# Six embedding products per layer computed inside two earlier norms and kept in DRAM

## The chip, the cores and the metric

The kernel runs on one core of one Trainium2 chip. The metric is the device time of one execution in microseconds, and less is better. One launch computes the whole network for a sequence of 512 tokens.

## The reference

`x` is 512 tokens of 1024 channels. A first block mixes tokens in three ways (gated linear attention, windowed attention, pooling), gates and adds the three, and projects; a conv feed-forward follows; behind each stands a norm of what was computed. A second network has an mLSTM layer, a per-layer embedding (PLE) addition, a shared key and value projection, a dilated attention layer, and another PLE addition. Cut to what the change touches:

```
x = x + rmsnorm(merged @ w_out, norm_mix_post)          # the norm of mixing
f = conv_ffn(rmsnorm(x, norm_ffn_pre), ...)
x = x + rmsnorm(f, norm_ffn_post)                       # the norm of the feed-forward
...
def ple_add(h, p_l, norm_g, w_gate, w_proj):
    gate = sigmoid(rms_norm(h, norm_g) @ w_gate)        # 1024 x 1024
    return h + (p_l @ w_proj) * gate                    # p_l is an input: 512 x 256
```

The product `p_l @ w_proj` depends on inputs alone.

## The kernel before, in words

Activations lie transposed, channels on partitions and 512 tokens along the free dimension, so 1024 channels are 8 tiles of 128x512. Every fp32 product is three fp32r matmuls: each operand is split into a high part (a rounded copy) and a low part (what the rounding left), and PE adds high times high, high times low and low times high (`passes`, L386). A block is a weight of 128x128; a tile with k blocks takes 3k matmuls of 512 columns.

All weights come through one stream. SP loads units of 8 blocks (512 KB) into 3 raw buffers (`Loads`, L299), ACT rounds a unit into `WH` (`High`), DVE subtracts to get `WL` (`Low`), both in 5 slots, and PE uses the units in the order in which `_layout` packed them. There is no planner: each engine runs its own program, written by hand, and all five walk the same list of tiles (`tile`, `first`, `tokens4`, `taken`). At each block an engine calls `prepare` (L200), which brings its share of the stream up to 3 units ahead (4 for ACT); so weights are prepared only between the other instructions of that engine, in its program order. `later` lets small pieces that were put off (norm sums, ropes) run at fixed points. PE has eight PSUM banks: a ring `mp` of 3, or 7 where the other uses rest, and `SB` for the side work.

Four stages matter here.

*A norm behind a projection* (`pe_post` L649, `v_post` L1056, `a_post` L1703). ACT copies the last product tile to SBUF and squares the copy, POOL adds the square to `SQS`, PE sums over partitions (`pe_columns`: 4 small fp32 products), ACT and DVE make the reciprocal root, PE spreads it over a tile (`pe_row`), ACT copies that to `RT`. Then DVE, for each of 8 tiles: scales `F` by `RT` into `TT` (L1067), adds it to `X` (L1070), and, one tile later, subtracts `HH` from the scaled `X` for the low part `HL` (`v_low`, L1030); ACT makes `HH` and the squares for the next norm, POOL adds them.

*The opening behind it* (`first`, L415, and `tokens4`, L428). The first tiles of the next projection run k-outermost over several banks, so PE can use tile k of `HH` and `HL` as soon as it is there: 6 up-projection tiles behind mixing, 4 value tiles behind the feed-forward.

*A residual* (`residual`, L840, L1357, L1892): 8 tiles of an output projection; DVE adds each to `X`, waits for ACT's `HH` of the same tile, and makes `HL` at once.

*The PLE stage* (`ple`, L845, L1372, L1906): 3 gate tiles k-outermost (`pg`), 4 embedding products (`pw`, 2 blocks each), then 5 gate tiles with the last 4 products between them. For each tile DVE multiplies by the norm row (`v_half_tanh`, L1039), ACT takes tanh, DVE multiplies by the product in PSUM, adds to `X`, waits for ACT's high part, makes the low part, and only then goes on. The second PLE stage has no high and low parts, as it is the end.

## Time and profile before

| what | value |
|---|---|
| median of 3 runs | 1577.84 us (1574.33 to 1579.94) |
| the profiled execution | 1574.86 us, span 1572.9 us |
| mean granted TensorE clock | 0.963 of full |
| busy: PE, DVE, ACT, POOL | 1467.1, 929.2, 594.9, 162.2 us |
| data moved | 123.78 MB read, 2.10 MB written |

Busy times are sums over the instructions of an engine, and PE's are modelled, so a busy PE isn't PE at its peak. Where an engine is not the one that others wait for, its idle time costs nothing. All times within the trace count from the start of the span.

### The profile page before, as it was taken

How to read it: one execution, taken by the hardware profiler on the slowest of the kernel's cores; microseconds unless marked ns; L12 is line 12 of the kernel's file. 1: busy time of each engine (PE TensorE's matmuls, PEld its weight loads, DVE VectorE, ACT ScalarE, POOL GpSimd, SP SyncE). 2: the span in 40 equal slices, each digit the busy share in tenths (PEclk: the TensorE clock that was granted, in tenths of full speed). 3: DMA queues.
4: the chain of work that ended last, by engine and by line, in shares of the span. 5: the costliest groups of instructions: out<-in, count | busy, mean ns of one | idle time of the engine just before them, and what ended most of it. 6: DMA issues, size and time to landing. Idle time of an engine off the chain costs nothing.

```text
span 1572.9 us, 17894 instructions
## 1 busy us (share of the span) xinstructions
PE 1467.1 (93%) x7104; PEld 1186.8 (75%) x7104; DVE 929.2 (59%) x1273; ACT 594.9 (38%) x892; POOL 162.2 (10%) x124
## 2 busy tenths in 40 slices
PE   6998989899998989999999899899999999998898
PEld 5876767678876768888888678577888778776676
DVE  5443756555343689617884458445455757887654
ACT  5232543433234323322323352334444443556441
POOL 3300010120212200000001210000001101110010
PEclk9999999999998999999999899899999999999899
DMA  6220212122341213332333122211233242111221
GB/s 210 81 68 27 96 53 68 54 68 70 119 147 54 81 50 110 123 94 80 97 101 100 51 69 83 78 54 54 61 104 103 70 125 77 54 54 41 66 82 54
DMA packets 35971, 127.03 MB, mean 81 GB/s; under 512 B 4128, under 2 KB 4784, under 8 KB 35888
## 3 DMA queue, kind: packets, MB, share of 16 engines
q1 hardware_dynamic: 35888, 125.89, 25.8%
q8 instruction: 56, 0.92, 0.2%
q14 instruction: 27, 0.22, 0.0%
HBM read 123.78 MB, written 2.10 MB: 80 GB/s over the span
## 4 chain that ended last, share of the span: by engine, by line
PE 47%; DVE 12%; ACT 5%; issue 2%; DMA 0%; POOL 0%; DVEq 0%; ACTq 0%; SPq 0%
PE ps L191 47%; DVE WL L145 2%; DVE TT L157 2%; DVE PB L145 1%; DVE QK L157 1%; ACT L188 1%; DVE SS L157 1%; DVE TH L145 1%; ACT SS L188 1%; DVE sm L163 1%; DVE X L145 1%; ACT TH L188 1%; DVE HL L157 1%; DVE CT L157 1%; ACT WH L175 0%
## 5 line engine op out<-in xcount | busy, mean ns | idle before, releaser
L191 PE MATMUL ps<-HH,WH 128*128 128x512 f32 x1208 | 496.6, 411 | 32.1 <-DVE WL L145 21.1
L191 PE MATMUL ps<-HH,WL 128*128 128x512 f32 x1208 | 478.7, 396 | 0.0
L191 PE MATMUL ps<-HL,WH 128*128 128x512 f32 x1208 | 478.6, 396 | 0.0
L145 DVE TENSOR_TENSOR WL<-raw,WH 128x1024 fp32r<-128x1024 f32 x222 | 294.1, 1332 | 82.6 <-ACT WH L175 74.3
L191 PEld LDWEIGHTS ps<-HH,WH 128*128 128x128 f32 x1208 | 232.0, 192 | 90.0 <-issue 22.0
L175 ACT CAST WH<-raw 128x1024 fp32r<-128x1024 f32 x222 | 230.2, 1043 | 167.0 <-PE ps L191 128.7
L191 PEld LDWEIGHTS ps<-HH,WL 128*128 128x128 f32 x1208 | 231.6, 192 | 50.8
L191 PEld LDWEIGHTS ps<-HL,WH 128*128 128x128 f32 x1208 | 232.5, 192 | 47.9 <-issue 2.0
L191 PE MATMUL ps<-PH,WH 128*128 128x512 f32 x432 | 174.3, 404 | 6.4 <-DVE TT L157 3.4
L191 PE MATMUL ps<-PL,WH 128*128 128x512 f32 x432 | 170.5, 395 | 0.0
L191 PE MATMUL ps<-PH,WL 128*128 128x512 f32 x432 | 170.4, 394 | 0.0
L145 POOL TENSOR_TENSOR SQS<-SQS,SQ 128x512 f32<-128x512 f32 x56 | 81.3, 1452 | 825.4 <-ACT SQ L188 824.5
L145 DVE TENSOR_TENSOR TH<-ps,RS 128x512 f32<-128x512 f32 x100 | 68.6, 686 | 75.7 <-PE ps L191 70.3
L191 PEld LDWEIGHTS ps<-PH,WH 128*128 128x128 f32 x432 | 82.4, 191 | 27.6 <-DVE TT L157 4.2
L191 PEld LDWEIGHTS ps<-PH,WL 128*128 128x128 f32 x432 | 82.5, 191 | 17.8
L191 PEld LDWEIGHTS ps<-PL,WH 128*128 128x128 f32 x432 | 82.6, 191 | 16.2
L188 ACT ACTIVATE TH<-TH 128x512 f32<-128x512 f32 x48 | 30.3, 632 | 111.0 <-DVE TH L145 111.0
L157 DVE SCALAR_TENSOR_TENSOR CT<-TH,cv,CT 128x511 f32<-128x511 f32 x88 | 66.1, 751 | 3.1
L188 ACT ACT_TABLE_LOAD x49 | 62.9, 1283 | 10.2 <-DMA X<-in_xT 6.2
L169 DVE RECIPROCAL sm<-sm 128x4 f32<-128x4 f32 (+1 forms) x60 | 10.1, 171 | 93.6 <-ACT sm L188 91.1
L157 DVE SCALAR_TENSOR_TENSOR HL<-X,cv,HH 128x512 fp32r<-128x512 f32 x48 | 48.7, 1024 | 22.8 <-ACT HH L188 22.8
L191 PE MATMUL ps<-WH,HH 128*128 128x512 f32 (+1 forms) x128 | 49.6, 387 | 12.9 <-DVE WL L145 8.6
(194 smaller groups left out, 1500.9 us busy)
## 6 DMA issues: line engine op xcount, KB each, us to landing
raw<-in_wall SPq DMA_DIRECT2D x222, 512.0 KB, 3.6
X<-in_xT SPq DMA_DIRECT2D x8, 512.0 KB, 6.1
out_T<-X SPq DMA_DIRECT2D x8, 256.0 KB, 2.0
pt<-in_pT SPq DMA_DIRECT2D x2, 512.0 KB, 3.9
DM<-in_dm SPq DMA_DIRECT2D x1, 640.0 KB, 4.4
CS<-in_cs SPq DMA_DIRECT2D x1, 512.0 KB, 5.3
plw<-in_plw SPq DMA_DIRECT2D x1, 256.0 KB, 7.6
lvm<-in_lvm SPq DMA_DIRECT2D x1, 192.0 KB, 8.0
```

The lines of the kernel that those rows point to most:

```text
L145: return self.put(None if self.e is None else self.e.tensor_tensor(out, x, y, op))
L157: return self.put(self.e.scalar_tensor_tensor(out=out, in0=x, scalar=s, in1=y, op0=op0, op1=op1))
L163: return self.put(None if self.e is None else self.e.tensor_reduce(out, x, AX_X, op))
L169: return self.put(None if self.e is None else self.e.reciprocal(out, x))
L175: return self.put(None if self.e is None else self.e.copy(out, x))
L188: return self.put(self.e.activation(out, x, f, **kw))
L191: return self.put(None if self.e is None else self.e.matmul(out, l, r, start=start, stop=stop, skip_group_check=True))
```

## The change

Six of the eight embedding products of each layer (`EARLY = 6`) move out of the PLE stages: those of layer 0 into the norm of mixing, those of layer 1 into the norm of the feed-forward. The embedding `p` is loaded and split early for that (`early`). ACT copies each product to SBUF (`PW`), SP writes the six to DRAM (`kept`, 1.5 MB a layer) and reads them back (`PWR`) in front of the PLE stage. In the two norms the last square goes straight to PE without POOL's addition, mixing squares straight from PSUM, DVE reads the norm row from PSUM, and `ahead` lets ACT and DVE prepare weights inside the loop. The opening behind mixing has 4 tiles and no longer 6. PLE stages lose their k-outermost opening, and residuals and PLE stages make the low part one tile later. `_layout` follows the new order; the number of units is the same.

```diff
+    def ahead(self, m, n):
+        at = (self.blk + n * max(m - 2, 0)) // 8
+        self.prepare(at, at + NW - 1)
...
+        pes = [at("pe0", [P, 2, T], F32, o2), at("pe1", [P, 2, T], F32, ar + 24576)]
+        PW = [at("PW0", [P, EARLY, T], F32, ar + 26112), at("PW1", [P, EARLY, T], F32, ar + 16384)]
+        PWR = at("PWR", [P, EARLY, T], F32, ar)
+        kept = nc.dram_tensor("kept", [2, P, EARLY, T], F32, kind="Internal").ap()
...
-        def pe_post(p, st):
-            pe_columns(p, (SB[4], ("nc", st)), [(SQS, S.pool, ("sqs", st, 7))], [free("sqs", st)])
+        def pe_post(p, st, layer):
+            p.tile(("pw", layer, 0), O_e[layer])
+            pe_columns(p, (SB[4], ("nc", st)), [(SQS, S.pool, ("sqs", st, 6)), (sq_(st, 7), S.act, ("sqs in", st, 7))],
+                       [free("sqs", st), free("Q", (st, 7))])
+            p.tile(("pw", layer, 1), O_e[layer])
             pe_row(p, SB[4], ("nr", st), col_("post", st), ("post col", st), [free("COL", ("post", st))])
+            for m in range(2, EARLY):
+                p.tile(("pw", layer, m), O_e[layer])
...
+            def ple(layer, H, st, nxt):
+                for m in range(EARLY, 8):
+                    p.tile(("pw", layer, m), O_p[layer], SB[m - EARLY])
+                p.soon.append(pe_norm(p, st))
                 for m in range(8):
+                    p.tile(("pg", layer, m), H)
                 if nxt:
                     p.soon.append(pe_norm(p, nxt))
...
-            p.first([("up", 0, j, o) for j in range(3) for o in range(2)], H_ffn, [p.next_bank() for _ in range(6)])
+            p.first([("up", 0, j, o) for j in range(2) for o in range(2)], H_ffn, [p.next_bank() for _ in range(4)])
...
-            p.tokens4([("vt", t) for t in range(4)], H_kv, [p.next_bank() for _ in range(3)] + [SB[0]], early=True)
+            p.tokens4([("vt", t) for t in range(4)], H_kv, [SB[2], SB[3], p.next_bank(), p.next_bank()], early=True)
...
         def v_post(v, st, F, post, nxt, gain):
+            v.tile(2)
             v_column(v, ("post col", st), col_("post", st))
+            for m in range(1, 3):
+                v.tile(2)
             for m in range(8):
+                v.ahead(m, 4)
                 v.take("T", (st, m))
-                v.wait_ge(S.act, "post row", st)
+                v.wait_ge(S.pe, "nr", st)
...
-                v.scalar_tensor_tensor(tt_(st, m), F[:, m, :], c(post, m), rt_("post", st), MUL,
+                v.scalar_tensor_tensor(tt_(st, m), F[:, m, :], c(post, m), ps("nr", st), MUL,
...
+                if 3 <= m < EARLY:
+                    v.tile(2)
...
+            def early(layer):
+                for k in range(2):
+                    hi, lo = O_e[layer][k][0:2]
+                    v.wait_ge(S.act, "pe hi", layer, k)
+                    v.wait_ge(S.early[layer], "early")
+                    v.tensor_tensor(lo, pes[layer][:, k, :], hi.bitcast(F32), SUB).then_inc(("pe", layer, k))
...
-                    v_low(v, nxt, m, gain, HH, HL)
-                v.soon.append(v_norm(v, nxt))
+                    if m:
+                        v_low(v, nxt, m - 1, gain, HH, HL)
+                v_low(v, nxt, 7, gain, HH, HL)
...
                     v_half_tanh(v, tg, st)
-                    if 1 <= m <= 4:
-                        v.tile(2)
+                    if nxt and m:
+                        v_low(v, nxt, m - 1, "norm_kv", PH, PL)
                     v.take("T", tg)
                     v.wait_ge(S.act, "tanh", tg)
-                    v.wait_ge(S.pe, *tw)
...
+                    if m < EARLY:
+                        v.wait_ge(S.again[layer], "again")
+                        v.scalar_tensor_tensor(tt_(*tg), th_(*tg), 1.0, PWR[:, m, :], ADD, MUL).then_inc(("pt", layer, m), free("TH", tg))
...
+        def a_keep(a, layer, m):
+            a.wait_ge(S.pe, "pw", layer, m)
+            a.copy(PW[layer][:, m, :], ps("pw", layer, m)).then_inc(("pw", layer, m), free("pw", layer, m))
...
             for m in range(8):
+                a.ahead(m, 4)
...
+                if m + 3 < EARLY:
+                    a.tile(2)
+                    a_keep(a, layer, m + 3)
...
+                a_square(a, "mix post", m, ps("f", m), ("sqs", "mix"))
                 a.copy(FA[:, m, :], ps("f", m)).then_inc(("f", m), free("f", m))
-                a.wait_ge(S.act, "f", m)
-                a_square(a, "mix post", m, FA[:, m, :], ("sqs", "mix"))
...
+            def keep(layer):
+                s.wait_ge(S.act, "pw", layer, EARLY - 1)
+                s.dma_start(kept[layer], PW[layer]).then_inc("kept", sig=S.kept[layer], by=16)
...
             s.dma_start(pts[layer], a_in["pT"][layer]).then_inc("p", sig=S.p[layer], by=16)
+            s.wait_ge(S.kept[layer], "kept")
+            s.dma_start(PWR, kept[layer]).then_inc("again", sig=S.again[layer], by=16)
```

`keep(0)` stands behind the opening's weights in SP's queue, `keep(1)` behind the value tiles'; `load_p`, whose lines end the diff, stands in front of each residual. SP also loads `p` twice more (0.5 MB each). ACT's and DVE's `head` and ACT's `early(1)` wait for the writes before they reuse the memory.

## Rows read from the trace of the kernel before

**Rows 1.** The page, busy us, share of the span and instructions of each engine
```profile
PE 1467.1 (93%) x7104; PEld 1186.8 (75%) x7104; DVE 929.2 (59%) x1273; ACT 594.9 (38%) x892; POOL 162.2 (10%) x124
```

**Rows 2.** Windows: us, busy us (xcount) of PE, PEld, DVE, ACT, POOL; granted clock, DMA share, GB/s
```profile
497.20:508.20 11.00, 3.28 (x17) 2.96 (x17) 3.79 (x7) 5.37 (x9) 1.26 (x1) 0.65 0.00 0
...
508.20:546.00 37.80, 35.86 (x144) 29.06 (x145) 27.05 (x25) 14.01 (x19) 11.30 (x7) 0.92 0.25 84
...
546.00:645.00 99.00, 91.68 (x404) 75.65 (x404) 86.30 (x121) 29.07 (x39) 0.00 (x0) 0.97 0.26 80
...
884.00:924.20 40.20, 29.65 (x114) 24.29 (x114) 29.05 (x30) 16.70 (x24) 12.53 (x8) 0.79 0.12 41
...
1200.50:1285.40 84.90, 80.86 (x361) 66.51 (x359) 47.46 (x49) 34.69 (x46) 10.71 (x8) 0.98 0.31 93
...
1503.10:1567.60 64.50, 59.96 (x256) 48.28 (x254) 28.65 (x36) 17.13 (x22) 3.94 (x3) 0.95 0.20 70
```

**Rows 3.** Timeline (start, us), norm behind w_out
```profile
491.79 0.59 ACT L175 COPY FA<-ps 128x512 f32<-128x512 f32 x1 [3.25 <-PE ps L191]
...
497.23 0.58 ACT L175 COPY FA<-ps 128x512 f32<-128x512 f32 x1 [3.25 <-PE ps L191]
...
498.55 1.26 POOL L145 TENSOR_TENSOR SQS<-SQS,SQ 128x512 f32<-128x512 f32 x1 [4.13 <-ACT SQ L188]
...
499.87 1.23 PE L191 MATMUL ps<-ones,SQS 128*128 128x1 f32 x8 [2.67 <-POOL SQS L145]
...
501.75 2.04 PE L191 MATMUL ps<-ident,sm 128*128 128x128 f32 x8 [0.66 <-DVE sm L169]
...
503.83 0.58 ACT L175 COPY RT<-ps 128x512 f32<-128x512 f32 x1 [2.44 <-PE ps L191]
...
504.52 0.75 DVE L157 SCALAR_TENSOR_TENSOR TT<-FA,cv,RT 128x512 f32<-128x512 f32 x1 [2.91 <-ACT RT L175]
```

**Rows 4.** Timeline, end of the opening that follows, and the up projections
```profile
524.88 3.49 DVE L157 SCALAR_TENSOR_TENSOR HL<-X,cv,HH 128x512 fp32r<-128x512 f32 x2
...
528.30 3.48 DVE L145 TENSOR_TENSOR WL<-raw,WH 128x1024 fp32r<-128x1024 f32 x3
...
549.55 0.69 DVE L145 TENSOR_TENSOR TH<-ps,RS 128x512 f32<-128x512 f32 x1 [2.03 <-ACT RS L175]
...
570.44 1.22 DVE L145 TENSOR_TENSOR WL<-raw,WH 128x1024 fp32r<-128x1024 f32 x1
...
571.80 0.76 PE L191 MATMUL ps<-HH,WH 128*128 128x512 f32 x1 [6.66 <-DVE WL L145]
```

**Rows 5.** Timeline, two matmuls in a row on PE, 2 us into that opening
```profile
510.04 0.63 PE L191 MATMUL ps<-HL,WH 128*128 128x512 f32 x1
...
510.46 0.63 PE L191 MATMUL ps<-HH,WL 128*128 128x512 f32 x1
```

**Rows 6.** Timeline, first embedding layer
```profile
1216.70 0.95 PE L191 MATMUL ps<-ones,SQS 128*128 128x1 f32 x8
...
1218.99 1.05 PE L191 MATMUL ps<-ident,sm 128*128 128x128 f32 x8
...
1250.12 0.69 DVE L145 TENSOR_TENSOR TH<-ps,RS 128x512 f32<-128x512 f32 x1 [0.22 <-PE ps L191]
...
1256.63 0.68 DVE L145 TENSOR_TENSOR TH<-ps,RS 128x512 f32<-128x512 f32 x1
...
1263.85 0.50 PE L191 MATMUL ps<-WH,PH 128*128 128x512 f32 x1 [1.53 <-DVE TH L145]
```

**Rows 7.** Timeline, last residual, POOL and DVE at once
```profile
1493.22 1.34 POOL L145 TENSOR_TENSOR SQS<-SQS,SQ 128x512 f32<-128x512 f32 x1 [3.04 <-ACT SQ L188]
1493.32 0.68 DVE L145 TENSOR_TENSOR X<-X,ps 128x512 f32<-128x512 f32 x1
```

**Rows 8.** The page, DMA issues: count, KB each, median us to landing
```profile
raw<-in_wall SPq DMA_DIRECT2D x222, 512.0 KB, 3.6
X<-in_xT SPq DMA_DIRECT2D x8, 512.0 KB, 6.1
```

More of the change, by code:

```diff
@@ L64, in __init__ @@
         self.p = [p0, p1]
+        self.early = [e0, e1]
+        self.kept = [kept0, kept1]
+        self.again = [again0, again1]
         self.work = [self.pe, self.dve, self.act, self.pool]
@@ L954, in pe_program @@
                     for o in range(2):
-                        if half == 0 and jj < 3:
+                        if half == 0 and jj < 2:
                             p.taken()
@@ L1533, in dve_program @@
                     v.tile(8)
+                if m == 4:
+                    early(0)
             v.mark("merged")
             v_post(v, "mix post", FA, "mix_post", "ffn", "ffn_pre")
-            v.first(8, 6)
+            v.first(8, 4)
             v.mark("fb")
@@ L1551, in dve_program @@
                     for o in range(2):
-                        if half == 0 and jj < 3:
+                        if half == 0 and jj < 2:
                             v.taken()
@@ L1567, in dve_program @@
                     v.tile(11)
+                    if half == 1 and m == 4:
+                        early(1)
                     if half == 1:
@@ L1843, in head @@
                 a.wait_ge(S.act, "acol")
+                a.wait_ge(S.kept[1], "kept")
                 if h:
@@ L1903, in residual, with ple @@
                     a_square(a, nxt, m, X[:, m, :], ("sqs", last))
-                a.soon.append(a_norm(a, nxt, use))
-            def ple(layer, nxt, last):
-                a.first(8, 3)
-                for m in range(4):
+            def ple(layer, st, nxt, last, use):
+                for m in range(EARLY, 8):
                     a.tile(2)
+                a.soon.append(a_norm(a, st, use))
                 for m in range(8):
-                    if m < 3:
-                        a.taken()
-                    else:
-                        a.tile(8)
+                    a.tile(8)
                     a_tanh(a, ("pg", layer, m))
-                    if 1 <= m <= 4:
-                        a.tile(2)
                     if nxt:
@@ L2018, in act_program, with early @@
                 a.activation(HH[:, m, :], X[:, m, :], ACT.Copy, scale=0.5).then_inc(("mg hi", m))
+            def early(layer):
+                for k in range(2):
+                    hi = O_e[layer][k][0]
+                    a.wait_ge(S.early[layer], "early")
+                    if layer:
+                        a.wait_ge(S.kept[0], "kept")
+                    a.copy(hi, pes[layer][:, k, :]).then_inc(("pe hi", layer, k))
             a.mark("fa")
@@ L2049, in act_program @@
                     for o in range(2):
-                        if half == 0 and jj < 3:
+                        if half == 0 and jj < 2:
                             a.taken()
@@ L2065, in act_program @@
                     a.tile(11)
+                    if half == 1 and m == 4:
+                        early(1)
                     if half == 0:
@@ L2323, in sp_program @@
                 s.tile(8)
-            s.first(8, 6)
+            for m in range(EARLY):
+                s.tile(2)
+            s.first(8, 4)
+            keep(0)
             for half in range(2):
-                for _ in range(22 - 6 * (half == 0)):
+                for i in range(22 - 4 * (half == 0)):
                     s.tile(8)
+                if half == 1:
+                    s.wait_ge(S.kept[0], "kept")
+                    s.dma_start(pes[1], a_in["pT"][1]).then_inc("early", sig=S.early[1], by=16)
                 for m in range(8):
                     s.tile(11)
+            for m in range(EARLY):
+                s.tile(2)
             s.tokens4(8)
+            keep(1)
             s.wait_mark("a")
@@ L2457, in _layout @@
         if half == 0:
-            side_by_side(*((up, j * P + o) for j in range(3) for o in (0, 2816)))
-        for j in range(half * 11 or 3, (half + 1) * 11):
+            side_by_side(*((up, j * P + o) for j in range(2) for o in (0, 2816)))
+        for j in range(half * 11 or 2, (half + 1) * 11):
             form(up, j * P)
```

105 lines of the change are left out of this document (50 added, 55 removed).

## The prediction

> **What bounds the kernel.** I began with the page's busy times: PE is busy 1467.1 of 1572.9 us and nothing else comes near [rows 1], so what matters is where PE waits or runs slowly. The list of waits and the timeline put most of that into few stages. I cut the span into windows at their borders, measured from the end of one projection to the start of the next use [rows 2]. The reader should see in them that the granted clock is 0.65 in the 11 us of the norm behind mixing, where PE does 3.3 us of work, and 0.79 in the whole stretch behind the feed-forward; and that DVE, not PE, is nearly full there (29.1 of 40.2 us) and is at 86.3 of 99.0 us in the first half of the up projections.
>
> **The pace.** Two tiles of 24 matmuls end 5.44 us apart [rows 3], so a matmul takes 0.227 us at the clock of 2.4 GHz. At 1.2 GHz two in a row start 0.42 us apart [rows 5]. The matmuls of the change are the same ones in another order. Six products are 36 matmuls, 8.2 us, in each layer. The change gains what PE's order fills or removes.
>
> **The norm of mixing, now.** The last tile of w_out ends at 497.2 [rows 3]. ACT copies (0.58), squares, POOL adds (1.26), and the sums start at 499.87, 2.7 us late. They take 1.23 and the row 2.04, both at the lower clock. ACT copies the row, DVE starts at 504.52. PE starts the opening only at 508.2. DVE's loop of 8 tiles runs until 524.88 + 3.49 = 528.4, so 23.9 us [rows 3, 4]. That is more than 24 instructions of 0.75: the last two take 3.49 together [rows 4]; seven are stretched like that, each while POOL adds.
>
> **The norm of mixing, after.** Product 0 fills 497.2 to 498.6; the last square goes first on ACT and is there by 497.9. The sums are twice as many, 2 x 0.95 at the full clock [rows 6], to 500.5. Product 1 to 501.8 covers the root, also if a weight cast and a table load keep it until 501.1. The row takes 1.05 [rows 6], to 502.9. DVE reads it from PSUM and starts 1.6 us earlier. Products 2 to 5 are 24 matmuls, to 508.3. The first low part is due by 506.8 (DVE's start plus the 3.5 us that it takes now), so PE doesn't stop, and its clock should not have fallen.
>
> DVE's loop has the same 24 instructions and, by `ahead`, four low weights (indices 4 to 7 from the first unit of the products; 0 to 3 are ready). Three of them take 3.48 us [rows 4], so 1.16 each and 4.6 together: the loop takes 28.5 us, to 531.4. ACT's additions (6 copies at 0.58, four casts) lie beside it: ACT is busy 14 of 37.8 us in the opening now [rows 2]. POOL loses one addition. The last k-step is 12 matmuls, 2.7 us, to 534.2. PE alone would be through 32 blocks (21.8 us) at 530.1, so **DVE becomes the bound of the opening** and PE stalls 4.1 us in pieces of up to 1.6, in front of the steps that a low weight delays. The next norm adds 2.7 as now, to 536.9.
>
> Now DVE has six tiles waiting for that norm. It works from 549.55 to 570.44 before it comes to a weight, and PE, with three units in hand (16.3 us), starves for 6.66 us until 571.80 and comes back at the lower clock [rows 4]. With four tiles DVE takes 20.9 x 4/6 = 13.9 us, and PE has 28 blocks, 3.5 units, 19.1 us. The starvation goes. What is late next is nothing in this stage: 18 tiles take PE 97.9 us, and DVE's work for all 22 is 86.3 us [rows 2]. It ends at 536.9 + 97.9 = 634.8 against 644.5: **9.7 us earlier**, with 8.2 us of products done besides.
>
> **The norm of the feed-forward.** The same steps: DVE starts 5.7 us in, 28.5 for its loop, 2.7 for the last step, 36.9 against 40.2 us [rows 2], so **3.3 us earlier**. DVE had done its weights behind the loop; now they come inside it.
>
> **The PLE stages.** In the first one a tile costs DVE 6.5 us (1250.12 to 1256.63), more than PE's 5.44: norm multiply, wait for tanh, two steps, wait for ACT's high part (0.8), low part, weight (2.3, beside POOL) [rows 6]. After the change the low part fills the wait for tanh and the wait for the high part is gone: 1.15 to 2.3 + 0.7 + 0.75 + 0.7 + 0.7, at most 5.2 us. PE bounds it. From the end of the residual: 2 products 2.7, norm 2.0, 8 tiles 43.5, value tiles 21.8, sums 0.95, together 71.0 against 84.9 us [rows 2]: **13.9 us**. Of these, 8.2 are the products; the rest are waits for DVE, the 1.5 us in front of 1263.85 among them [rows 6]. The p0 norm loses its cover of 24 matmuls, but its sums stand after half of gate tile 0, 5.4 us behind the residual, and DVE, ACT and POOL need 0.69 + 0.72 + 0.62 + 1.34, 3.4 us.
>
> In the second, 2.7 + 2.0 + 43.5 = 48.2 against 64.5 us [rows 2]: **16.3 us**. Here the three banks of the present opening were held by DVE, which is 6.5 us for two residual tiles where PE needs 5.44; with the wait for ACT gone it needs 5.0 to 6.0, and 5.4 us of other PE work stand behind it. The tail is the same.
>
> **Edits costed at nothing.** The early split of `p` (4 instructions of 0.6 us a layer on ACT and DVE) lies under w_out and the down projection, where PE's tiles take 5.44 and 33 x 0.227 = 7.5 us; uncovered it would be 1.3 us each. The four transfers of 1.5 MB are unlike any row; the nearest give 86 to 145 GB/s (0.52 MB in 6.1 or 3.6 us) [rows 8], so 11 to 18 us each. The writes stand behind weights that are already issued. In front of a residual `p` and the products (2.1 MB, 14.5 to 24.4 us) stand ahead of the next weights, with 3 units, 16.3 us, in hand. I take the fast value, since the raw loads are the same kind: no stall. The slow end is 8.1 us at each place. The products are needed only behind the residual, which is 8 x 5.44 = 44 us in layer 0 and half of that in layer 1.
>
> **The sum.** 9.7 + 3.3 + 13.9 + 16.3 = 43.2 us. From it I take 2 us for a fall of the clock in one of the openings' stalls (14 matmuls at 0.42 cost 2.9; stalls of 1.5 us leave it up [rows 6], one of 6.66 does not), so 41. The profiled execution took 1574.86 us, 0.2% under the median, so 1533.9 for it and **1536.8** beside 1577.84.
>
> A rule that bears on DVE's loop: while POOL added, a DVE instruction that reads PSUM kept its 0.68 us [rows 7]. The Trainium skill, "SBUF — State Buffer", "Who interferes with whom", says that a VectorE instruction with at most one SBUF input does not contend with GpSimd. The trace agrees. Two of the seven slow ones in the loop are scalings that will read PSUM, at 1.05 us each; by the rule the sum would be up to 4 us better, by the row's pattern (the next instruction waits instead) nothing.
>
> **Rivals.** (a) *The openings fall into the lower clock.* Each has three or four stalls now; if each of six costs 2.9 us, it is 15 more than I took: 1552. Against it: gaps of 1.5 us left the clock up. The Trainium skill, "TensorE: Matmul & The Clock Gate", "A second HAM failure mode: psum-queue depth-cycling", tells of a kernel whose short idles between groups made the clock swing; the trace doesn't show that for gaps this short.
> (b) *The order of the low parts shortens nothing*, so PLE 0 stays at 6.5 us a tile: 8 x 1.06 = 8.5 us, 1545. For it: DVE is the releaser there now. Against it: 0.8 us of each tile is a wait for ACT.
> (c) *The reloads starve PE*, at the slow rate: 2 x (8.1 + 2 for the clock) = 20 us, 1557. The same mechanism turns to **slower than before** when each place costs 20.5 us, which is 2.1 MB in 36.8 us, under 57 GB/s. At 45 GB/s it is 30 us each, 1597. Against it: the slowest row is 86, and the page's raw loads land in 3.6 us.
> (d) *It doesn't do what it says*: DVE's backlog behind the openings eats their 13 us and DVE-bound PLE stages the rest but for the last one: about 1573.
>
> **Chances.** Forecast 0.64, its own range 1531 to 1543; (a) 0.12; (b) 0.11; (c) 0.07 short of the turn, 0.03 beyond it; (d) 0.03. The 80% range takes the forecast, (a) mostly and (b): 1529 to 1554. About 0.3% is what a measurement of this kernel can tell from no change. Faster 0.94; same 0.03; slower 0.03.
>
> **What would show it.** PE without a gap from the last tile of w_out to the end of product 5; DVE's loop of 28 us; no gap behind the four up tiles; norm multiplies 5.44 us apart in PLE 0. I am wrong if PE stalls more than 5 us in an opening, if the clock in one is under 0.9, or if a weight load lands over 16 us after a reload was issued.

## The result and the profile after

Measured beside each other on one chip, the changed kernel takes **1534.69 us** (median of 4 runs, 1533.44 to 1535.64) where the kernel before takes 1576.09 (4 runs, 1574.14 to 1579.94): 0.9736 of its time, with a 95% interval of 0.9718 to 0.9754. The forecast was 1536.8, range 1529 to 1554. The profiled span went from 1572.9 to 1533.0 us.

The page of the changed kernel, first the engines [rows 1], then its DMA issues [rows 8]:

```profile
PE 1453.6 (95%) x7120; PEld 1179.2 (77%) x7120; DVE 913.5 (60%) x1277; ACT 602.2 (39%) x908; POOL 171.3 (11%) x122
...
kept<-PW SPq DMA_DIRECT2D x2, 1536.0 KB, 7.6
...
PWR<-kept SPq DMA_DIRECT2D x2, 1536.0 KB, 7.6
```

PE does the same work in 13.5 us less busy time (about 35 matmuls fewer run at the lower clock, 0.42 us apart instead of 0.23, which is half of it), and the other 26 us are waits that are gone. (The sixteen matmuls more are the second sums of the two norms.) The windows of the changed kernel, with the columns of [rows 2]:

```profile
497.00:507.80 10.80, 10.80 (x61) 9.32 (x60) 5.07 (x9) 8.52 (x14) 0.00 (x0) 1.00 0.09 36
507.80:533.20 25.40, 23.05 (x99) 17.78 (x98) 22.44 (x22) 12.60 (x19) 11.13 (x7) 1.00 0.32 91
533.20:633.70 100.50, 99.84 (x450) 82.92 (x449) 86.92 (x119) 30.76 (x40) 0.00 (x0) 1.00 0.33 103
633.70:876.80 243.10, 241.31 (x1058) 199.27 (x1057) 139.70 (x174) 69.51 (x86) 9.25 (x6) 0.99 0.34 102
876.80:910.90 34.10, 33.54 (x160) 27.33 (x158) 27.18 (x31) 19.74 (x30) 10.79 (x7) 1.00 0.28 71
910.90:997.00 86.10, 76.31 (x337) 61.91 (x335) 53.77 (x70) 30.92 (x41) 0.00 (x0) 0.94 0.31 102
1191.50:1262.20 70.70, 70.70 (x325) 58.92 (x325) 41.38 (x49) 33.53 (x45) 10.44 (x8) 1.00 0.33 98
1479.30:1527.70 48.40, 48.36 (x220) 39.65 (x219) 25.57 (x32) 13.42 (x18) 2.33 (x2) 1.00 0.23 71
```

PE fills the norm behind mixing completely (10.80 of 10.80 us, where it had 3.28 of 11.00 [rows 2]) and the granted clock is 1.00 in every stage that the change meant to reach. It also fills both embedding stages. But one row is out of line: 910.9 to 997.0 has PE busy 76.3 of 86.1 us at a clock of 0.94, and that stage had not been part of the forecast. Put beside the windows of before, border by border, the whole span comes out (the forecast column is before the 2 us that the forecast held back for a fall of the clock):

```
stage                                     before   after    change   forecast
norm behind mixing, ups of half 0          147.8   136.7     -11.1      -9.7
downs of half 0, half 1                    239.0   243.1      +4.1       0
norm of the feed-forward, first V tiles     40.2    34.1      -6.1      -3.3
rest of attention stage a, to the heads     78.4    86.1      +7.7       0
heads and first residual                   197.9   194.5      -3.4       0
first embedding stage                       84.9    70.7     -14.2     -13.9
second layer's attention                   217.7   217.1      -0.6       0
second embedding stage                      64.5    48.4     -16.1     -16.3
ahead of the norm of mixing, and the tail  502.5   502.3      -0.2       0
sum                                       1572.9  1533.0     -39.9     -43.2
```

(The border at 645.0 [rows 2] lies 0.5 us behind the last matmul of that stage, so PE's own share of the first two lines is -10.6 and +3.6.) The sum is near the forecast one, but two losses nobody had forecast, 11.8 us, stand against gains larger than forecast.

One of these gains is in no edited stage, the 3.4 us between the heads and the first residual. Its windows, of the kernel before and of the changed one:

```profile
1002.60:1200.50 197.90, 195.94 (x889) 154.42 (x890) 99.59 (x136) 78.24 (x125) 8.06 (x6) 0.95 0.22 65
```

```profile
997.00:1191.50 194.50, 191.68 (x889) 151.74 (x890) 91.88 (x135) 78.28 (x124) 9.58 (x6) 0.97 0.24 76
```

The same 889 matmuls take PE 4.3 us less, with a granted clock of 0.97 and not 0.95, while its idle time grows from 2.0 to 2.8 us. So these 3.4 us are the clock, not waits; why it is higher here, no run shows.

**The openings.** The timeline of the changed kernel (start, us; in brackets the idle time before it and what ended it), to be read against [rows 3, 4, 5]:

```profile
502.59 0.75 DVE L163 SCALAR_TENSOR_TENSOR TT<-FA,cv,ps 128x512 f32<-128x512 f32 x1 [1.70 <-PE ps L197]
...
508.38 2.32 DVE L151 TENSOR_TENSOR WL<-raw,WH 128x1024 fp32r<-128x1024 f32 x1
...
513.76 1.59 POOL L151 TENSOR_TENSOR SQS<-SQS,SQ 128x512 f32<-128x512 f32 x1 [1.91 <-ACT SQ L194]
...
514.13 0.73 DVE L163 SCALAR_TENSOR_TENSOR TT<-FA,cv,ps 128x512 f32<-128x512 f32 x1
514.89 1.00 DVE L151 TENSOR_TENSOR X<-X,TT 128x512 f32<-128x512 f32 x1
...
524.07 0.47 PE L197 MATMUL ps<-HH,WH 128*128 128x512 f32 x1 [1.35 <-DVE HL L163]
...
526.69 1.62 DVE L163 SCALAR_TENSOR_TENSOR HL<-X,cv,HH 128x512 fp32r<-128x512 f32 x2
...
642.35 0.50 PE L197 MATMUL ps<-PH,WH 128*128 128x512 f32 x1 [1.79 <-DVE PL L151]
...
643.63 0.63 PE L197 MATMUL ps<-PH,WL 128*128 128x512 f32 x1
...
646.62 0.59 PE L197 MATMUL ps<-PH,WH 128*128 128x512 f32 x1
647.04 0.40 PE L197 MATMUL ps<-PL,WH 128*128 128x512 f32 x1
```

DVE starts at 502.59, 1.9 us earlier than before, and ends its loop at 528.3: 25.7 us, where the forecast was 28.5. The scaling of 514.13, which reads PSUM, keeps its 0.73 us beside POOL's addition of 513.76, and the addition of 514.89, which reads SBUF twice, takes 1.00 where one free of POOL takes 0.69; POOL's addition ends at 515.35, so it looks as if DVE waits for what is left of it. The last rows are the first loss. In the first down tile PE is 1.79 us early for DVE's last low part PL, and 1.3 us after it resumes, eight matmuls follow each other at 0.42 us instead of 0.23 (643.63 to 647.04). That is 1.8 + 8 x 0.19 = 3.3 of the 3.6 us. (The traces of low_undo, row_copy, open6, again4, gate3 and bank below have the same wait, 1.63 to 1.86 us, no_ahead has 0.44 and early4 none; the slow matmuls behind it are in bank alone.)

Why DVE is late shows in its list of waits over the up projections (533.2 to 633.7 us):

```profile
DVE PL L151 <- ACT PH L181: 6.9, 10, 0.7
DVE sm L175 <- ACT sm L194: 3.8, 1, 3.8
DVE TH L151 <- ACT RS L181: 2.0, 1, 2.0
```

DVE is busy for 86.9 of these 100.5 us, waits 12.7 us for ACT, and not once for PE. So it has no time in this stage to catch up: it comes out of the opening behind PE and stays behind to the last tile.

**Stage a.** The second loss, in the same timeline:

```profile
967.84 0.68 DVE L151 TENSOR_TENSOR TH<-ps,RS 128x512 f32<-128x512 f32 x1
968.58 0.80 PE L197 MATMUL ps<-WH,HH 128*128 128x512 f32 x1 [4.66 <-DVE TH L151]
...
973.90 0.68 DVE L151 TENSOR_TENSOR TH<-ps,RS 128x512 f32<-128x512 f32 x1
974.63 0.80 PE L197 MATMUL ps<-WH,HH 128*128 128x512 f32 x1 [4.41 <-DVE TH L151]
```

These are the second four value tiles of the attention. They don't wait for data: each needs a PSUM bank, and the bank is one that DVE has yet to read (PE starts 0.06 and 0.05 us after DVE's reads at 967.84 and 973.90 end). The banks are handed out in a ring, and the change takes twelve products out of later stages and puts them into earlier ones, so the ring stands elsewhere when stage a begins. Nobody edited this line.

### The profile page after: what moved, and what is told of

It is laid out like the page before. It is cut to its first block, busy times and chain, and to the rows that moved or that the text cites. A ratio compares the mean times of both kernels' runs of the same rounds, so it can differ in the third digit from the quotient of the medians.

```text
span 1533.0 us, 17910 instructions
## 1 busy us (share of the span) xinstructions
PE 1453.6 (95%) x7120; PEld 1179.2 (77%) x7120; DVE 913.5 (60%) x1277; ACT 602.2 (39%) x908; POOL 171.3 (11%) x122
## 4 chain that ended last, share of the span: by engine, by line
PE 72%; DVE 18%; ACT 6%; issue 3%; DMA 1%; POOL 1%; DVEq 0%; SPq 0%; ACTq 0%
PE ps L197 71%; DVE WL L151 4%; DVE CT L163 2%; DVE TT L163 1%; DVE TH L151 1%; ACT L194 1%; DVE PB L151 1%; DVE QK L163 1%; DVE SS L163 1%; DVE sm L169 1%; DVE CT L158 1%; ACT SS L194 1%; DVE HL L163 1%; ACT PH L181 1%; DVE gqks L151 1%
## 5 line engine op out<-in xcount | busy, mean ns | idle before, releaser
L197 PE MATMUL ps<-HH,WH 128*128 128x512 f32 x1208 | 494.2, 409 | 18.1 <-DVE WL L151 12.7
L151 DVE TENSOR_TENSOR WL<-raw,WH 128x1024 fp32r<-128x1024 f32 x222 | 281.7, 1272 | 75.5 <-ACT WH L181 74.8
L197 PEld LDWEIGHTS ps<-PL,WH 128*128 128x128 f32 x426 | 81.5, 191 | 16.1
L194 ACT ACTIVATE HH<-X,cv 128x512 fp32r<-128x512 f32 x48 | 34.7, 723 | 47.4 <-DVE X L151 47.4
```

The costliest lines, as they stand in the source:

```text
L151: return self.put(None if self.e is None else self.e.tensor_tensor(out, x, y, op))
L194: return self.put(self.e.activation(out, x, f, **kw))
L197: return self.put(None if self.e is None else self.e.matmul(out, l, r, start=start, stop=stop, skip_group_check=True))
```

## The experiments

Each kernel is the changed one with one edit, except the first. The ratios are to the kernel before, measured beside it on the same chip, with 95% intervals. Stage times are cut at landmarks that every trace has: *dn0*, from the last copy of `FA` to the first of `FB` (opening, ups and first down tile); *va0*, from the last addition of `FB` to the first copy of `VA`; *heads*, from there to the heads' first row product; *res a*, to the last addition of the residual; *ple 1*, to the next layer's first `VT`; *res z*, to the last addition of the second residual; *end*, from there.

```
us           dn0    va0   heads  res a  ple 1  res z   end    span
before     154.9   41.6   77.0  197.9   85.3  221.6  65.4  1572.9
after      145.8   35.4   84.8  194.5   71.2  218.6  51.7  1533.0
low_only   157.8   41.9   76.7  199.2   81.2  217.6  62.4  1566.4
low_undo   145.9   35.4   84.5  196.5   71.2  221.2  53.3  1535.3
row_copy   148.3   38.8   85.0  194.4   71.2  218.9  51.7  1536.2
early4     143.3   37.2   76.9  195.8   75.7  221.0  55.9  1536.5
open6      151.0   35.4   85.3  196.0   71.2  221.2  51.6  1538.6
no_ahead   146.2   35.7   85.8  195.6   71.2  218.6  51.7  1534.9
again4     145.8   35.4   84.6  203.8   71.2  227.3  55.3  1553.0
bank       145.9   35.4   73.5  195.6   71.2  218.6  51.7  1522.4
dnfirst    164.1   35.4   85.1  195.3   71.2  218.2  51.7  1528.8
gate3      145.9   35.3   84.6  196.5   75.2  219.1  53.9  1540.0
both       164.1   35.4   73.5  197.4   71.2  219.6  51.7  1523.6
both5      164.1   35.3   73.6  197.5   71.2  217.2  51.6  1518.4
```

A stage that an edit doesn't touch can differ by up to 3 us between these kernels: *res a* goes from 194.4 to 197.5, *dn0* is 2.9 us longer in low_only than before, and *res z* is 219.6 and 217.2 in *both* and *both5*, which are the same kernel. In *res a* 7 to 24 matmuls run at the lower clock, in places that move. *va0*, *ple 1* and *end* are steadier, within 0.4 us where nothing touches them. So a stage's change is read only where it is over that or where a row of the timeline carries it.

### The order of the low parts: alone, and taken back

Alone, in the kernel before (each low part one tile later):

```diff
                     v.tensor_tensor(X[:, m, :], X[:, m, :], ps("res", st, m), ADD).then_inc(("x " + nxt, m), free("res", st, m))
-                    v_low(v, nxt, m, gain, HH, HL)
+                    if m:
+                        v_low(v, nxt, m - 1, gain, HH, HL)
+                v_low(v, nxt, 7, gain, HH, HL)
...
+                    if nxt and m:
+                        v_low(v, nxt, m - 1, "norm_kv", PH, PL)
                     v.take("T", tg)
```

> The kernel before, with nothing but the low parts of residuals and embedding stages made one tile later. My account (the wait for ACT's high part inside DVE's chain, 0.8 us a tile, made DVE the bound): the first embedding stage, 84.9 us from the end of the residual to the end of the value tiles, has 240 matmuls, 96 for the values and 3 us of norm, 79.3 us in all, so it can gain up to 5.5, and the second, 64.5 us for 240 matmuls and 2.0, up to 8: 6 to 13 us less together, 1563 to 1570. Rival (the order of the low parts does nothing by itself, only the moved products count): 1575 to 1578.

Measured: 1568.3 us (1567.54 to 1568.57), ratio 0.9933 [0.9913, 0.9954]. Some 10.6 us by the ratio and 6.5 by the traces. *ple 1* gives 4.1 us, *res z* and *end* together 7.0; *dn0*, untouched, is 2.9 longer. So in the kernel before, the order alone shortens the embedding stages.

The same edit taken out of the changed kernel:

> The kernel after, with the low parts back in their old place. My account: the 8 tiles of the first embedding stage go back from 5.44 to 6.5 us, 8.5 us longer, and in the last residual DVE needs 6.5 us for two tiles where PE needs 5.44, of which part is hidden behind the two products; 8.5 to 13 us more, 1543 to 1548. Rival (with the products gone from the stage DVE has room enough, since it no longer meets them): within 2 us of 1534.7.

Measured: 1539.62 us (1537.06 to 1542.34), ratio 0.9753 [0.9729, 0.9776]: 2.3 us slower than with the order by the spans, 4.9 by the medians, and the intervals of the two ratios overlap. It lies between the two ranges expected. The first embedding stage is 71.2 us as with the order. The timeline of this kernel, two gate tiles of that stage and the next norm:

```profile
1219.21 0.68 DVE L151 TENSOR_TENSOR TH<-ps,RS 128x512 f32<-128x512 f32 x1
...
1225.70 0.68 DVE L151 TENSOR_TENSOR TH<-ps,RS 128x512 f32<-128x512 f32 x1
...
1485.37 1.34 PE L197 MATMUL ps<-ones,SQS 128*128 128x1 f32 x8 [4.12 <-POOL SQS L151]
```

DVE takes 6.5 us a tile again, as before [rows 6], and with the new order 5.44 (below). PE doesn't feel it, and has no wait in this stage: eight tiles let DVE fall some 8 us behind, and it seems that there are banks enough to hold that. My reading of [rows 6], that a tile's DVE time sets the stage, was wrong for the changed kernel. The loss is at the second residual, where the sums wait 4.12 us for a chain that begins with DVE's last addition; the changed kernel has no wait there, and *res z* and *end* together are 4.2 us longer.

### The norm's row: read from PSUM, or from a copy

```diff
-                v.wait_ge(S.pe, "nr", st)
+                v.wait_ge(S.act, "post row", st)
...
-                v.scalar_tensor_tensor(tt_(st, m), F[:, m, :], c(post, m), ps("nr", st), MUL,
-                                       MUL).then_inc(("post", st, m), *([free("nr", st)] * (m == 7)))
+                v.scalar_tensor_tensor(tt_(st, m), F[:, m, :], c(post, m), rt_("post", st), MUL,
+                                       MUL).then_inc(("post", st, m), *([free("RT", ("post", st))] * (m == 7)))
```

> The kernel after, but DVE reads the norm row of the two post norms from SBUF, where ACT copies it first, as before. The copy puts 0.6 us in front of DVE's loop. If a DVE instruction with one SBUF input never waits for POOL, and one with two does, the seven slow instructions of a loop come back in full: the loop goes from 25.7 to about 28.5 us, PE's stalls in the opening behind mixing from 2.3 to about 5 us, and the total is 3 to 7 us more (1538 to 1542). If the slowing has to do with time alone (a POOL addition costs DVE 1 us whatever it runs), only the copy is seen: 0.6 us twice, 1535 to 1536.

Measured: 1542.64 us (1537.94 to 1543.32), ratio 0.9765 [0.9741, 0.979]; by the span 3.2 us slower. The timeline of this kernel, two of the three scalings in the mixing norm that meet an addition of POOL, and that addition for the second:

```profile
509.42 1.78 DVE L163 SCALAR_TENSOR_TENSOR TT<-FA,cv,RT 128x512 f32<-128x512 f32 x1
...
524.88 1.59 POOL L151 TENSOR_TENSOR SQS<-SQS,SQ 128x512 f32<-128x512 f32 x1 [3.83 <-ACT SQ L194]
...
525.24 1.78 DVE L163 SCALAR_TENSOR_TENSOR TT<-FA,cv,RT 128x512 f32<-128x512 f32 x1
```

Each of the three takes 1.78 us where the scaling from PSUM takes 0.73; the other five take 0.74. DVE's loops, first scaling to last low part, go from 25.7 to 27.6 us and from 24.3 to 27.2, *dn0* grows by 2.5 and *va0* by 3.4 us. The traces agree with the rule that the forecast quoted and left out of its sum (the Trainium skill, "SBUF — State Buffer", "Who interferes with whom"): with one operand in PSUM the scaling keeps its 0.73 us beside POOL. The next instruction takes 0.3 us more, and not all that the scaling was spared.

### How many products go into the norms

```diff
-EARLY = 6
+EARLY = 4
```

> The kernel after with four early products a layer and not six; the other two of each layer go back to the embedding stages. There they cost 12 matmuls, 2.7 us each layer. In the openings PE starts 2.7 us sooner. My account (DVE's loop sets the end of the opening): little of that is gained, since PE's stalls of 2.3 and 0.6 us in the two openings grow by nearly as much; 3 to 5 us more in total, 1538 to 1540. Rival (PE's work sets the end of the opening, so a product costs the same in either place): 1534 to 1536.

Measured: 1537.03 us (1536.39 to 1538.28), ratio 0.9735 [0.9711, 0.9759], the same as with six. That is short of the 1538 to 1540 that my account gave and above the rival's range, and neither foresaw what is in it. *ple 1* is 4.5 us longer and *end* 4.2, where 12 matmuls more are 2.7. In *ple 1* a wait of 1.49 us for DVE, which the changed kernel hasn't got, makes up most of the difference. In the openings my account holds: PE's waits there grow from 2.3 and 0.6 us to 4.2 in each, against the 2.7 us by which PE starts sooner, and *va0* is 1.8 us longer with less work in it. (*res z*, +2.4, is within what it varies by.) Against that, *dn0* is 2.5 us shorter, 1.8 of it the wait at the first down tile that this kernel hasn't got, and *heads* 7.9. The timeline of this kernel in stage a:

```profile
988.14 1.12 PE L197 MATMUL ps<-row,ident 4*128 4x512 f32 x2 [3.26 <-ACT VA L194]
```

The two waits of 4.66 and 4.41 us for banks are gone: with four banks fewer taken ahead of it the ring stands elsewhere. What is left is the wait for `VA` that the kernel before has too (3.4 us, below). This pointed to the bank experiment below.

### How many up tiles are opened at once

Six tiles in mixing's opening instead of four (the same edit on every engine and in the order of the weights):

```diff
-            p.first([("up", 0, j, o) for j in range(2) for o in range(2)], H_ffn, [p.next_bank() for _ in range(4)])
+            p.first([("up", 0, j, o) for j in range(3) for o in range(2)], H_ffn, [p.next_bank() for _ in range(6)])
```

> The kernel after with an opening of six up-projection tiles behind mixing and not four. My account (DVE meets six waiting tiles behind the norm and comes to a weight only after 20.9 us, while PE has 3.5 units, 19.1 us): PE starves again, though less than the 6.7 us of before, for 2 to 7 us and a fall of the clock behind it; but PE has no stall in the opening, which is 18 matmuls a step: 0 to +6 us, most likely 3 more, 1535 to 1541. Rival (the four tiles only matter for the end of the opening, nothing behind it): 1532 to 1534, better by the opening's 2.3 us of stalls.

Measured: 1541.07 us (1540.42 to 1542.12), ratio 0.9773 [0.9749, 0.9798]. *dn0* is 5.2 us longer, and the timeline of this kernel has the starvation of [rows 4] back, nearly to the number:

```profile
566.06 0.80 PE L197 MATMUL ps<-HH,WH 128*128 128x512 f32 x1 [6.39 <-DVE WL L151]
```

### Without the low weights in the loop

```diff
             for m in range(8):
-                v.ahead(m, 4)
                 v.take("T", (st, m))
```

(and the same line on ACT)

> The kernel after without the preparation of weights inside the loops of the two post norms. My account: PE has the units ready at the start of a loop and stands when they are used up, until DVE has left the loop: blocks 12 to 31 of the opening, so 5 us after its start, at about 516; DVE's loop is 4 to 5 us shorter and ends at 524, then weights come at 1.2 us each: PE stands 8 to 9 us in each opening, with the clock down behind it. The end of each opening is the end of the loop plus five k-steps of 2.7 us: 538 against 533.2. So 5 us each and 1 to 2 for the clock, 10 to 14 in all: 1545 to 1549. Rival (the loop is DVE's bound and is shorter without the weights, so that it evens out): within 3 us.

Measured: 1536.85 us (1533.52 to 1538.3), ratio 0.9741 [0.9718, 0.9765]: no difference that can be told. The rival's range, within 3 us, was right, and my account of 10 to 14 us wrong. DVE's loops are 21.9 and 20.8 us instead of 25.7 and 24.3, and the weights are made elsewhere, at the cost of two waits in this kernel's timeline:

```profile
534.81 2.04 PE L197 MATMUL ps<-ident,sm 128*128 128x128 f32 x8 [3.52 <-DVE sm L175]
...
904.98 0.50 PE L197 MATMUL ps<-WH,HH 128*128 128x512 f32 x1 [1.31 <-DVE WL L151]
```

The same work stands inside or behind the loop, and PE meets it either way.

### The transfers: four reads instead of one

The read of the products is done four times over, one after another; the data is the same.

```diff
                 s.wait_ge(S.kept[layer], "kept")
+                for r in range(3):
+                    s.dma_start(PWR, kept[layer]).then_inc(("once", r), sig=S.again[layer], by=16)
+                    s.wait_ge(S.again[layer], "once", r)
                 s.dma_start(PWR, kept[layer]).then_inc("again", sig=S.again[layer], by=16)
```

> The kernel after with the reload of the kept products done four times in a row, each waiting for the one before, in front of each residual: 4 x 7.6 = 30.4 us and not 7.6 that the weights stand behind. My account (three units, 16.3 us, are in hand there): 14 us of stall at each of the two places and up to 2 us for the clock, 28 to 32 us more, 1563 to 1567. If the stock at hand is larger than I took it (raw buffers, units rounded and split ahead), less: each further unit is 5.4 us less at each place. If reloads disturbed weights even now, the single one would show as a stall too, and the step would be the full 22.8 us twice, 1580.

Measured: 1553.69 us (1553.23 to 1554.8), ratio 0.9852 [0.9831, 0.9873]. The page of this kernel has the transfers, its timeline the stalls:

```profile
PWR<-kept SPq DMA_DIRECT2D x8, 1536.0 KB, 6.8
```

```profile
1185.17 0.80 PE L197 MATMUL ps<-PH,WH 128*128 128x512 f32 x1 [4.11 <-DVE X L151]
...
1501.27 1.87 PE L197 MATMUL ps<-ones,SQS 128*128 128x1 f32 x8 [8.35 <-POOL SQS L151]
```

PE stalls where expected, but three more reads, 20 to 23 us, cost only 9.3 us at the first place (*res a*) and 12.3 at the second (*res z* and *end*). So more time was in hand than the 16.3 us of weights that I used. In the changed kernel the two weight loads issued right behind the first read (1152 to 1160 us) land 8.0 and 7.5 us after their issue, and its PE waits for no weight there. One read of 7.6 us stands well inside the stock, and rival (c) has no room here.

### The bank ring in stage a

The four value tiles take the four banks that were used longest ago:

```diff
+            oldest = [p.next_bank() for _ in range(4)]
             p.mp = [b for b in p.mp if b not in SB[0:4]]
-            p.tokens4([("va", 1, t) for t in range(4)], H_a, [p.next_bank() for _ in range(3)] + [SB[0]])
+            p.tokens4([("va", 1, t) for t in range(4)], H_a, oldest)
```

> The kernel after, with the second set of value tiles (va 1) in the four banks that were used longest ago, where the kernel takes the three of the ring and the first side bank, two of which DVE has not read yet: PE stands 4.66 and 4.40 us there at 964 to 975 and its clock is down behind it. My account (an accident of the bank ring, turned by the moved products): the stalls go; what is left is the wait for ACT's copies in front of the heads, 3.4 us before and 0.8 now. 4 to 8 us less, 1527 to 1531. Rival (DVE's backlog is the bound of this stage, and the wait only moves to the head products): within 1 us.

Measured: **1524.8 us** (1523.85 to 1528.08), ratio 0.9672 [0.9649, 0.9695]. *heads* goes from 84.8 to 73.5 us, more than was expected. PE's waits there, from the list of waits, first of the changed kernel (950 to 1000 us; us in total, times, longest), then of this one (940 to 990):

```profile
PE ps L197 <- DVE TH L151: 9.1, 2, 4.7
PE ps L197 <- ACT VA L194: 0.8, 1, 0.8
```

```profile
PE ps L197 <- DVE WL L151: 0.7, 2, 0.3
PE ps L197 <- ACT VA L194: 0.5, 1, 0.5
```

The kernel before has one wait of 3.4 us for `VA` in the same place, so this edit beats that one too:

```profile
PE ps L191 <- ACT VA L188: 3.4, 1, 3.4
```

The window of this kernel between the same landmarks as the changed kernel's 910.9 to 997.0 shows the clock kept as well. The 9.1 us of waits and the low clock behind them (a granted clock of 0.94 there, 1.00 here) make the 11.3:

```profile
910.50:985.40 74.90, 74.25 (x338) 60.28 (x336) 53.36 (x70) 27.19 (x37) 0.00 (x0) 1.00 0.33 106
```

### The first down tiles side by side

The first four down tiles of half 0 take each step of their input in turn, so that they need the last low part late (the same on the other engines and in the order of the weights):

```diff
+                if half == 0:
+                    p.first([("dn", 0, m) for m in range(4)], O_ffn[0], [p.next_bank() for _ in range(4)])
+                for m in range(4 * (half == 0), 8):
                     p.tile(("dn", half, m), O_ffn[half])
```

> The kernel after, with the first four down-projection tiles of the first half k-outermost over four banks. In the kernel after, the first down tile reaches its last k-step 6.8 us behind the up projections and waits 1.79 us for DVE's last low part, at 640.6, and the clock is down for nine matmuls (1.8 us). k-outermost the last step comes after 27 us. My account: this gives back the 3.7 us that the stretch from the up projections to the end of the down projections lost against the kernel before: 3 to 4 us less, 1530.5 to 1532. Rival (DVE's lag comes back as a wait for one of the four banks at the start of the down tiles): within 1 us.

Measured: 1531.09 us (1530.55 to 1532.35), ratio 0.9712 [0.9686, 0.9737]. The first copy of `FB` comes later in this order, so *dn0* must be read together with the stretch behind it, up to the last addition of `FB`: 375.6 us against 379.3, 3.7 us less: the loss at the first down tile, taken back whole. (The intervals of the two ratios overlap; the stage carries this, not the total.) Against the kernels that have the wait without the slow matmuls (low_undo and gate3, 377.8) it is 2.2 us, the wait of 1.8 and little else.

### Gate tiles side by side in the embedding stages

```diff
+                p.first([("pg", layer, m) for m in range(3)], H, [p.next_bank() for _ in range(3)])
                 for m in range(8):
-                    p.tile(("pg", layer, m), H)
+                    if m < 3:
+                        p.taken()
+                    else:
+                        p.tile(("pg", layer, m), H)
```

This puts back the kind of opening that the change took out of the embedding stages.

> The kernel after with the k-outermost opening of three gate tiles back in both embedding stages, which the kernel before had; the products stay where they are after. low_undo left the first embedding stage at 71.2 us although DVE took 6.5 us a tile there, so DVE's chain is not what the stage lost; the opening is the suspect: the norm row comes only after three gate tiles, DVE then has three tiles waiting and PE no free bank. If that was what the stage lost besides the products' 8.2 us (14.1 us gained in all): about 5 us more in the first embedding stage and 5 or more in the second, 1540 to 1546. If the wait came from the products' own banks between the gate tiles (4 to 7 in the order of before), which this kernel hasn't got: PE stands only from the end of the sums to the first norm multiply, 1 to 3 us a stage, 1536 to 1541.

Measured: 1542.9 us (1541.84 to 1545.03), ratio 0.9789 [0.9773, 0.9805]. *ple 1* is 4.0 us longer, *end* 2.2: between what the two accounts gave a stage, 5 us and 1 to 3. In the timeline of this kernel (the first stage, then the second):

```profile
1212.15 1.13 PE L197 MATMUL ps<-ident,sm 128*128 128x128 f32 x8 [0.66 <-DVE sm L175]
...
1214.75 0.71 PE L197 MATMUL ps<-HH,WH 128*128 128x512 f32 x1 [1.47 <-DVE TH L151]
...
1507.15 0.50 PE L197 MATMUL ps<-HH,WH 128*128 128x512 f32 x1 [1.47 <-DVE TH L151]
```

Each stage has two short waits, 0.66 and 1.47, 2.1 us together; the first also has seven matmuls at the lower clock behind them. So this part of the change is worth 2 to 4 us a stage.

### Both repairs together

The edits of the bank ring and of the first down tiles in one kernel:

> The change of banks and the k-outermost down tiles together. If both waits are independent the gains add up: 7 to 12 us less than the kernel after, 1523 to 1528. If one feeds the other (a DVE backlog carried along), less than their sum.

Measured: 1525.08 us (1521.3 to 1527.11), ratio 0.9668 [0.9642, 0.9694], no better than the bank edit alone in the total. In their own stages both keep what they give alone (*heads* 73.5; 375.6 for *dn0* and the stretch behind it), but *res a* is 3 us longer than in the changed kernel. The same kernel again, in five runs:

> The same kernel as in the run called both, timed in more rounds. If the two gains add up and the first timing was blurred by where the clock falls elsewhere in the kernel, its ratio to the kernel before is 0.964 to 0.966 (the ratio of bank, 0.9672, less 3.7 us); if they don't, it stays at 0.967.

Measured: **1520.84 us** (5 runs, 1520.24 to 1524.3), ratio 0.9655 [0.9639, 0.9671], span 1518.4. The timeline of this kernel in the heads shows what takes back part of the gain, waits for DVE's and ACT's results that PE now comes to sooner:

```profile
982.50 1.77 PE L197 MATMUL ps<-QK 128*128 128x512 f32 x4 [0.53 <-ACT VA L194]
...
985.80 1.00 PE L197 MATMUL ps<-QK 128*128 128x256 f32 x4 [1.53 <-DVE Wt L163]
...
1046.87 0.95 PE L197 MATMUL ps<-QK 128*128 128x256 f32 x4 [0.88 <-DVE Wt L163]
```

With one more of 0.89 they are 3.8 us, where the changed kernel has one of 0.93, and one of 0.78 in front of the heads. This is the fastest version, 14 us below the changed kernel and 55 below the one before. Its interval still overlaps that of the bank edit alone, so that the second repair adds to the first is shown by the stages, not by the totals.

## Why the prediction was right, and where it was not

**The forecast time was right, and so was the kind of cause**: products in the norm, four tiles instead of six, no opening in the embedding stages. That the time came out within 2.1 us was also luck: 11.8 us of losses that it didn't have were made up by gains that it had too small or not at all. Point by point:

- *The norm of mixing, 9.7 us*: 10.6 by PE's own ends. The timeline shows the start (502.6, forecast 502.9), PE without a gap to the end of product 5, and the starvation gone; the open6 run shows that the four tiles did that, worth 5 to 6 us (*dn0* 5.2, the span 5.6).
- *"The loop takes 28.5 us"*: mis-sized, 25.7, by two errors of opposite sign. I charged 1.05 us of contention for each of seven instructions as before, and in the changed kernel's timeline one low part still takes 1.78 us and three additions take 1.0, and no scaling is slow. But I priced the low weights at 1.16 us each, and two of the four, beside POOL, take 2.3. The operand in PSUM alone is worth 1.9 us of the loop (row_copy). "DVE becomes the bound of the opening" holds all the same, but with 2.3 us of waits, not 4.1.
- *The norm of the feed-forward, 3.3 us*: 6.1, for the same reason: the loop is 24.3 us (27.2 with the row in SBUF).
- *"From it I take 2 us for a fall of the clock"*: none fell in an opening (1.00 in both). It fell where I had forecast no wait, at the first down tile (1.5 us) and in stage a. (Its price was off a little too: 14 matmuls at 0.42 and not 0.227 us cost 2.7 us, not 2.9.)
- *"What is late next is nothing in this stage"*: the step that failed. I compared the sums of the stage, 97.9 us for PE and 86.3 for DVE. But DVE's 86.3 are busy time alone; with 12.7 us of waits for ACT its chain fills the stage. It enters behind PE, is still behind at the end, and the first down tile needs its last output. 3.6 us here, 1.8 of them the wait and the rest a clock that falls in some kernels only; the dnfirst run takes both away.
- *Stage a was not in the sum at all.* Its code is unchanged, but its banks come from a ring that the moved products turn. 7.7 us, and the bank run takes away all of it and 3.5 us more. This was the largest error, hidden in the total by openings better by 4 us, a clock term of 2 that the openings didn't need, and the 3.4 us of clock between the heads and the first residual.
- *The embedding stages, 13.9 and 16.3 us*: 14.2 and 16.1. The sums held because PE really has no gap there. The working of the first held in part. 8.2 us are the products. Of the rest, 5.7, the kernel before has 4.0 us as two waits for DVE, that in front of 1263.85 [rows 6] and this one, which has six matmuls 0.42 us apart behind it, another 1.2 us:

```profile
1227.99 0.80 PE L191 MATMUL ps<-PH,WH 128*128 128x512 f32 x1 [2.46 <-DVE TT L157]
```

  So "the rest are waits for DVE" was right for the kernel before. What was wrong is the reason, DVE's 6.5 us a tile. Two things take most of it away, each without the other: the order in the kernel before (low_only, 4.1 us), and the products and the opening out of the stage without the order (low_undo, 71.2 us as with it). The opening put back costs 4.0 (gate3). The timeline of the changed kernel shows DVE with time to spare, waiting 1.5 us for PE at a tile, and its norm multiplies 5.44 us apart, as forecast:

```profile
1217.88 0.69 DVE L151 TENSOR_TENSOR TH<-ps,RS 128x512 f32<-128x512 f32 x1 [1.50 <-PE ps L197]
...
1223.32 0.69 DVE L151 TENSOR_TENSOR TH<-ps,RS 128x512 f32<-128x512 f32 x1 [1.49 <-PE ps L197]
```

- *The transfers*: 1536 KB in 7.6 us is 207 GB/s, faster than the bounds of 11 to 18 us that I took from smaller ones, and hidden.
- *The rivals*: (a) no clock fell in an opening; but its counter, that gaps of 1.5 us leave the clock up, doesn't hold everywhere (last section). (b) The order does shorten something, in the kernel before (low_only) and at the second residual (low_undo), but in the changed kernel's first embedding stage it shortens nothing, as (b) says; what fails is (b)'s price, 8.5 us for 6.5 us a tile, which PE doesn't feel. (c) refuted by again4; (d) refuted by the total. The signs of being wrong did not come: PE's waits in an opening were 2.3 us in all, the clock there 1.00, and no weight load landed late behind the first read.

Three things stay open: what moves *res a*, *res z* and *dn0* by up to 3 us between kernels that are alike there; why the clock was higher between the heads and the first residual of the changed kernel; and why *end* of early4 is 1.5 us longer than its added matmuls. No run was made for any of them.

## What to carry to other kernels

When work is moved, follow what it takes along without being named: here a ring of banks turned by twelve products cost a later, unedited stage 8 to 11 us. Compare engines at the point of hand-over and not by the sums of a stage; an engine that leaves an opening behind the other may still be behind at the stage's last tile. Count an engine's waits for a third engine as part of its chain; its busy time leaves them out. And an engine slower per tile than PE can cost nothing while tiles are few, as DVE did here at 6.5 us a tile in a stage of eight, so try the short stage before believing the rate.

## What the hardware showed that I had not expected

- A DVE scaling with its row operand in PSUM took 0.73 us beside a POOL addition, the same with both tiles in SBUF 1.78 us; the two-SBUF addition behind the former took 1.00 instead of 0.69. Moving one operand shortened loops of 27.6 and 27.2 us to 25.7 and 24.3.
- The same gap in PE's work, 1.8 us in front of the first down tile, was followed by eight matmuls at 1.2 GHz (0.42 us each) in two kernels (the changed one, 1.79, and bank, 1.84) and by none in five others (1.63 to 1.86 us: low_undo, row_copy, open6, again4, gate3). So these traces don't tell from such a gap alone whether the clock falls, and 1.5 us in a stage may be this and nothing else. In gate3 the gap of 1.47 us was followed by seven such matmuls in the first embedding stage and by none in the second. I had set the danger only at gaps like that of 6.66 us, and taken it that gaps of 1.5 us leave the clock up.
- Transfers of 1536 KB through one queue took 7.6 us both to and from DRAM, 6.8 in the median when repeated, so 207 to 231 GB/s, where the weights' 512 KB took 3.6 us.
